# A two-block kernel with eight experts: the list buffer moved behind the work area, and the last expert's rows scattered by TensorE

## The reference, cut to what matters

```
xt = xn.reshape(-1, d)
logits = (xt @ w_router).astype(jnp.float32)
top_vals, top_idx = lax.top_k(logits, TOP_K)          # 2 of 8 experts
top_w = jax.nn.softmax(top_vals, axis=-1)
combine = sum over the two of one_hot(top_idx) * top_w
y = 0
for e in range(N_EXPERTS):
    y = y + combine[:, e:e+1] * swiglu(xt, w_gate[e], w_up[e], w_down[e])
h = h + y                                             # then rmsnorm, then block two
```

## Time and profile before

| | us |
|---|---|
| median of three runs | 2692.67 |
| lowest, highest | 2691.4, 2695.11 |
| profiled execution, its own time | 2696.5 |
| its span, first to last instruction | 2694.4 |
| TensorE busy | 2529.3 (94%) |
| VectorE busy | 2008.3 (75%) |
| ScalarE busy | 1237.7 (46%) |
| GpSimd busy | 286.4 (11%) |
| DMA | 788.32 MB, mean 293 GB/s |

### The profile page before, as it was taken

How to read it: one execution, slowest core, us unless ns; L and a number is a source line. 1 busy time by engine, 2 the same in 40 slices (tenths; PEclk the granted TensorE clock), 3 DMA queues, 4 the chain that set the end, 5 groups by cost and what they waited for, 6 DMA issues and landing times.

```text
span 2694.4 us, 33145 instructions
## 1 busy us (share of the span) xinstructions
PE 2529.3 (94%) x12345; PEld 1981.4 (74%) x12345; DVE 2008.3 (75%) x2983; ACT 1237.7 (46%) x1250; POOL 286.4 (11%) x303
## 2 busy tenths in 40 slices
PE   9999999999999999999999997999999987787787
PEld 7898999899788888888888886888896543333332
DVE  5765654864888898889889894537656878888875
ACT  1454331263778777777777783124532111021111
POOL 0000000000000000000000000000003443333331
PEclk9999999999999999999999998999999999888899
DMA  7553554551999999999999996432658999999997
GB/s 219 168 196 110 188 180 119 164 161 60 343 373 378 368 383 368 376 371 377 377 372 382 364 385 213 146 110 63 193 171 344 422 420 422 421 422 422 421 421 310
DMA packets 339200, 788.32 MB, mean 293 GB/s; under 512 B 22288, under 2 KB 154512, under 8 KB 306064
## 3 DMA queue, kind: packets, MB, share of 16 engines
q1 hardware_dynamic: 298352, 504.99, 53.4%
q0 software_dynamic: 39600, 278.41, 25.4%
q10 hardware_dynamic: 1136, 3.43, 0.3%
HBM read 778.92 MB, written 7.86 MB: 292 GB/s over the span
## 4 chain that ended last, share of the span: by engine, by line
PE 76%; DMA 14%; DVE 4%; issue 3%; ACT 3%; POOL 0%; DVEq 0%; SPq 0%; ACTq 0%; POOLq 0%
DMA dense_weights<-in_peer_rows,work 12%; PE banks L810 12%; PE banks L812 12%; PE banks L811 12%; PE banks L622 6%; PE banks L685 5%; PE banks L1228 5%; PE banks L644 4%; PE banks L648 4%; PE banks L645 4%; PE banks L1191 2%; PE banks L921 1%; PE banks L554 1%; DMA squares<-in_peer_rows,work 1%; ACT weight_tiles_high L1489 1%
## 5 line engine op out<-in xcount | busy, mean ns | idle before, releaser
L2319 DVE TENSOR_TENSOR weight_tiles_low<-weight_tiles,weight_tiles_high 128x2048 fp32r<-128x2048 f32 x335 | 763.1, 2288 | 99.1 <-ACT weight_tiles_high L1701 97.3
L1701 ACT ACTIVATE weight_tiles_high<-weight_tiles 128x2048 fp32r<-128x2048 f32 x332 | 636.2, 1918 | 193.4 <-DMA weight_tiles<-in_moe_w_down 73.1
L1228 PE MATMUL banks<-dense_weights,work 128*128 128x512 f32 x952 | 463.0, 640 | 107.5 <-DVE work L2721 107.5
L1228 PEld LDWEIGHTS banks<-dense_weights,work 128*128 128x128 f32 x952 | 188.9, 204 | 369.9 <-issue 214.9
L810 PE MATMUL banks<-weight_tiles_high,gathered_parts 128*128 128x512 f32 x896 | 352.7, 394 | 1.3 <-DVE gathered_parts L2330 1.3
L812 PE MATMUL banks<-weight_tiles_high,gathered_parts 128*128 128x512 f32 x896 | 349.3, 390 | 0.0
L811 PE MATMUL banks<-weight_tiles_low,gathered_parts 128*128 128x512 f32 x896 | 348.9, 389 | 0.0
L2711 DVE CUSTOM_DVE_ANT_0 dense_weights<-dense_weights,banks 128x1024 f32<-128x1024 f32 x238 | 285.4, 1217 | 70.5 <-DMA dense_weights<-in_peer_rows,work 69.2
L1468 POOL DMA_INDIRECT dense_weights<-in_peer_rows,work x238 | 223.7, 940 | 702.9 <-DVE work L2688 331.2
L1986 DVE TENSOR_TENSOR weight_tiles_low<-weight_tiles,weight_tiles_high 128x2048 fp32r<-128x2048 f32 x85 | 194.1, 2289 | 130.1 <-ACT weight_tiles_high L1489 129.9
L1907 ACT ACTIVATE work<-work,small 128x2 f32<-128x2 f32 x129 | 38.1, 295 | 538.3 <-DVE work L2711 529.1
(11 more groups left out here) (445 smaller groups left out, 3833.0 us busy)
## 6 DMA issues: line engine op xcount, KB each, us to landing
weight_tiles<-in_moe_w_gate SPq DMA_DIRECT2D x112, 1024.0 KB, 7.0
weight_tiles<-in_moe_w_up SPq DMA_DIRECT2D x112, 1024.0 KB, 6.7
weight_tiles<-in_moe_w_down SPq DMA_DIRECT2D x112, 1024.0 KB, 6.0
weight_tiles<-in_w_in SPq DMA_DIRECT2D x38, 1024.0 KB, 5.8
weight_tiles<-in_w_xkv SPq DMA_DIRECT2D x16, 1024.0 KB, 5.6
weight_tiles<-in_ffn_w_gate SPq DMA_DIRECT2D x11, 1024.0 KB, 5.3
weight_tiles<-in_ffn_w_up SPq DMA_DIRECT2D x11, 1024.0 KB, 5.3
weight_tiles<-in_ffn_w_down SPq DMA_DIRECT2D x11, 1024.0 KB, 4.9
```

The costliest lines, as they stand in the source:

```text
L1228: mm = pe.matmul(halves[half], diag[(first + j) % 8], pair_row(first + j)[:, 1, half * 512:(half + 1) * 512], start=False, stop=end and j ...
L1701: act.activation(high_tile(j), raw_tile(j), ACT.Copy).then_inc(g.high, 1)
L2319: dve.tensor_tensor(low_tile(j), raw_tile(j), high_tile(j).bitcast(F32), ALU.subtract).then_inc(g.split, 1)
```

## The change

Two things are changed. First, `lists` is placed behind `work` and not ahead of `small`. `small` thereby starts at 172,832 and `work` at 173,888, both 64 bytes lower than before.

Second, the eighth indirect addition to `y_tokens` is left out, and the sum of the other seven is loaded while the last expert runs. TensorE transposes the one-hot matrix of the last expert's slots (`weighted_now`) to `put`, transposes `y_rows` as before, and multiplies `ye` by `put` into four more banks; VectorE copies `put` and adds eight banks to the residual in place of four.

```
-        lists = sb("lists", [P, 16])
         ...
         work_parts = sb("work_parts", [P, WORK], F32R)
+        lists = sb("lists", [P, 16])

@@ TensorE, after the loop over the experts
+            transposes("v", "put", [(b * P, weighted_now[:, b, :]) for b in range(TB)])
             pe.wait_ge(y_loaded, 16)
             for i in range(KT // 2):
                 transposes("v", ("y", i), [...])
+            pe.wait_ge(dve_took, G.took["put"])
+            for i in range(KT // 2):
+                if i % 2 == 0:
+                    pe.wait_ge(act_took, G.took["down", i // 2] + (N_EXP - 1) * G.takes["a"])
+                bank = G.begin("v", ("scatter_last", i))
+                for j in range(2):
+                    mm = pe.matmul(bank[:, j * SEQ:(j + 1) * SEQ], ye[:, (2 * i + j) * P:(2 * i + j + 1) * P], put, start=True, stop=True)
+                G.end(mm)

@@ SyncE
-            sp.wait_ge(y_done, 16 * (CLEARS + N_EXP))
+            sp.wait_ge(y_done, 16 * (CLEARS + N_EXP - 1))
+            sp.wait_ge(group_done, G.after["gather", KT // 2 - 1] + (N_EXP - 1) * G.in_turn)
             sp.dma_start(y_rows, y_tokens[0:SEQ, :]...).then_inc(y_loaded, 16)

@@ GpSimd, in the loop over the experts, behind the gather
+                if e == N_EXP - 1:
+                    break

@@ VectorE, after the experts
-            for i in range(KT // 2):
-                ready(("y", i))
-                s = hF[:, 2 * i:2 * i + 2, :]
-                take(dve.tensor_tensor(s, pair(bank_of(("y", i))), s, ALU.add))
+            ready("put")
+            take(dve.tensor_copy(put, bank_of("put")[:, 0:SEQ]))
+            for name in ("y", "scatter_last"):
+                for i in range(KT // 2):
+                    ready((name, i))
+                    if name == "scatter_last":
+                        dve.wait_ge(dve_took, G.took["y", i])
+                    s = hF[:, 2 * i:2 * i + 2, :]
+                    take(dve.tensor_tensor(s, pair(bank_of((name, i))), s, ALU.add))
```

More of the change, by code:

```diff
@@ L253, in two_blocks @@
         router = sb("router", [P, KT, N_EXP])
-        lists = sb("lists", [P, 16])
-        x_tokens = nc.dram_tensor("x_tokens", [SEQ, D], F32).ap()
-        y_tokens = nc.dram_tensor("y_tokens", [CLEARS * P, D], F32).ap()
         small = sb("small", [P, 256])
@@ L261, in two_blocks @@
         work_parts = sb("work_parts", [P, WORK], F32R)
+        lists = sb("lists", [P, 16])
+        x_tokens = nc.dram_tensor("x_tokens", [SEQ, D], F32).ap()
+        y_tokens = nc.dram_tensor("y_tokens", [CLEARS * P, D], F32).ap()
         def view(off, *shape, extra=False):
```

## The result

The changed kernel takes 2672.18 us, the median of four runs (2667.4 to 2673.12), beside 2692.28 for the kernel before in the same comparison: 20.1 us less, ratio 0.992 with a 95% interval of 0.9903 to 0.9937, that is 17 to 26 us. Two later comparisons of the unedited kernel gave 0.991 (0.9896 to 0.9924) and 0.9918 (0.9906 to 0.9931). 2669.5 was forecast. The profiled execution took 2673.09 (span 2671.3), 23.4 less than that of before.

A forecast was written before the change was run, and what follows sets the result against it. TensorE was taken to bound the kernel up to the DMA-bound PEER stage, DMA close behind in the experts. Gains of 11.7 + 11.2 + 0.3 = 23.2 us took the 2692.67 us median to 2669.5, range 2660 to 2682.

The forecast's parts named there:

- Down product: Experts' down matmuls: stationary operand comes to a multiple of 128 bytes, pitch falls from 233 to 227 ns, 8.1 us gained.
- Moving operands: Split products' moving operands in `work_parts` leave multiples of 128: 1.2 us gained in the dense feed-forward, 4.1 us elsewhere.
- `mem_high` as stationary operand: L766 and L767, 256 matmuls: the operand goes to 64 past a multiple of 128, 1.7 us lost.
- The placement in all: Moving `work` by 64 bytes, all its gains and losses in the matmuls' pitch summed: 11.7 us gained.
- The seam: Behind the last expert: VectorE's last addition ends at 1657.5 us instead of 1668.67, 11.2 us gained.
- What is late next: After the seam: VectorE's branch and L2438 to about 1664.6 us, ScalarE's branch showing, L1009 left at 6.65 us.
- The pad: `pad_v` goes, with one transpose and a copy; the last `keysT` group no longer waits for the copy: 0.3 us gained.
- placement without effect: Rival: pitch differs for a reason of the products themselves, only seam and pad gain: 2681.2 us, chance 0.12.
- DMA takes over: Rival in the experts: the down product's 8.1 us turn into TensorE waits for tiles; 2677.6 us, chance 0.08.
- slower: Rival: operands of `work_parts` cost 6.6 ns more per matmul at the new start; 7.2 us slower, 2699.9 us, chance 0.04.
- the pitch belongs to the form of the product: Rival on the matmuls' pitch: bank alternation and order of the products, not start addresses, set it; placement gains nothing, chance 0.12.

The follow-up runs named there:

- e1: The kernel before with only `lists` moved behind `work`, the old seam kept: 2679.68 us against 2693.32, ratio 0.995.
- e3: The kernel before with the experts' hidden values moved to a multiple of 128 bytes, the dense hidden values to 64 past one: ratio 0.9986.
- e7: The changed kernel with gathered tokens, experts' hidden values and dense hidden values at 0 past a multiple of 256: 2692.71 us.
- e5: The changed kernel with the experts' gathered tokens and hidden values at 64 past a multiple of 256: 2678.97 us, ratio 0.9935.
- e8: The changed kernel run again, unedited: 2669.9 us, ratio 0.991 against the kernel before.
- e4: The changed kernel without the overflow passes and their four branches: 2665.61 us against 2693.32 for the kernel before, ratio 0.9891.
- e6: The changed kernel with gathered tokens, experts' hidden values and dense hidden values at 192 past a multiple of 256: 2696.93 us.
- e9: The changed kernel with offsets set so every moving activation of the split products starts at 192 past 256: 2678.69 us beside 2671.05 unedited.
- e2: The changed kernel with `lists` back in its old place, the last expert still scattered by TensorE: 2685.87 us against 2693.32, ratio 0.9969.

## Why the prediction was right, point by point

- **Down product, 8.1 us**: right in size (8.0 in the profile, 8.1 in e1's), and DMA kept up, as argued: a window in the down stretch of the changed kernel has 369 GB/s with a share of 1.00. But the reason given was wrong, and the size was in part luck. I divided the starts by 128; e3 and e7 show a multiple of 128 at 232.3 to 232.7 ns, and e5 shows 64 past one at 229.0. The changed kernel's hidden values come to lie at 128 past 256, where the gathered tokens lie; at 0 the same argument would have promised 8 us and given 1.
- **Moving operands, 1.2 + 4.1 us**: the dense product gave 1.2. The other 960 matmuls gave 3.5 by their pitch in the profile after: `mem_high` from 119.8 to between 113.3 and 117.8 ns from one group of matmuls to the next, `y_low` and `merged_low` from 118.7 to 113.3, `attended_high`, `o_low` and `hl_high` from 120 to 117.8. The last are not bound to 117.8: in e1, with the same addresses, `attended_high` and `o_low` ran at 113.4. And the 117.5 ns that I took as the dense feed-forward's own is not: of the twelve profiles with `x_high` at 64, six run its first product at 117.8 and six at 113.4.
- **`mem_high` as stationary operand, 1.7 us lost**: wrong in sign. L766 and L767 went from 119.9 to 116.3 ns, 0.9 us gained. The 6.6 ns were the price of 192, and `mem_high` went from 128 to 64. Why that gains stays open: with 512 columns e5 shows 64 to be 1.7 ns dearer than 128, so the table of the experts' operands does not carry over to these 256 columns.
- **The placement in all**: 11.7 forecast, 13.6 us by e1's medians. The stages before the experts differ by up to 8 us between executions of kernels equal there (L811 of the experts starts at 677.2 in e8, 678.3 in e1, 682.7 in the changed kernel, 685.5 in e4), 4.7 of them by the pitch of the dense first product, so no single profile settles the last 2 us. The Trainium skill's rule ("TensorE: Matmul & The Clock Gate", "Back-to-back issue gap"), whose gap goes by columns alone, is contradicted for these float32 parts by 227.3 to 233.3 ns for the same 512 columns at one clock; the measurement decides.
- **The seam, 11.2 us**: 12.2 came. VectorE's last addition ended 6.5 us behind the start of the last down matmul (1644.24), 6.9 forecast. Its path was the one foreseen, but for one miscount: a float32 matmul is two rows of the trace, so the scatter's eight are sixteen, 3.47 us, and not 1.7; VectorE waited 0.17 us for each of the last two pairs.
- **What is late next** was mis-stated. I had VectorE's branch, L2438 and a slow second sum; TensorE's own branch (4.5 us, hidden before behind the waits of the other engines) came first, and it was the first sum that ran at 1.2 GHz (5.93 us for 3.69 before), the second at 2.4. I had ScalarE's branch show as well, and it did not: the first square started 3.1 us behind `ye`, released by VectorE's addition. From the last addition's end to L622 it is 17.6 us where it was 18.2, so the error cancelled. e4 shows TensorE's gap and the slow first sum as the branch's price.
- **The pad, 0.3 us**: it went, and nothing came of it. From the first transpose behind the product ahead of it to the next product there are 5.3 us before and 5.2 after; that product waits for the copy of the first `keysT` bank.
- **The clock in the second block**: not foreseen; 2.0 us lost against the profile of before. That 23.1 us of span stand beside 23.2 forecast is in part chance: 8.0 + 12.2 + 4.9 ahead of the experts, less 2.0. The medians differ by 20.1 us.
- The rivals: "placement without effect" is refuted by e1, "DMA takes over" by the expert stage, "slower" by both. The rival that the pitch belongs to the form of the product is refuted by e1 and e6 together.

**Left open**: what sets the moving side to 113.4 or 117.8 ns in executions of one kernel, and why the cross-attention's queries kept 113.3 in every profile with `x_high` at 64 and had 117.8 in e9's at 192; why `mem_high` as stationary operand gained; and whether the new seam itself brings the low clock at the two places (low there in eight of its nine profiles without fillers, in one of three with the old one), which would explain part of why e2's median gained 7.5 us when its seam is 12.7 shorter. A build with a longer or shorter seam in steps was not tried.

## What to carry to other kernels

Read the pitch from start to start, by operand, and not busy time: a step of 6 ns was hidden in rows that all say "busy", and 64 bytes of an unrelated buffer turned it on. When a DMA round trip at a seam is replaced by on-chip work, list what every engine does once between the two, branches too, because what was hidden behind the round trip is next. Before trusting a rule about addresses, move the operand to all four places, not to the one that fits, and profile the unedited kernel more than once: a product that changes its pitch between two executions of one kernel says nothing yet of the edit.

## What the runs showed that I had not expected

At a never-taken branch over a long body TensorE stood 4.5 us and VectorE 5.9, and removing all four branches with their bodies took 6.9 us off the seam. The stationary operand's start has a price modulo 256 (229.0, 227.3, 233.3, 232.3 ns at 64, 128, 192, 0, with the moving tile at 128). The same kernel at the same addresses ran a product of 1056 matmuls at 117.8 ns in one profile and at 113.4 in two. Right behind thirty-two records of 16 columns, with TensorE "busy" all the time, the granted clock was 1.2 GHz in nine of twelve profiles; with 128-column matmuls between them it stayed at 2.4 in the one profile taken.
